# Stick-breaking mixer with query rows in the partitions and reversed scans for the later sums, in a two-layer streaming encoder

## Reference

```python
def sb_attend(q, q_pos, k, v):
    z = einsum('bqhd,bshd->bhqs', q, k) * HEAD_DIM ** -0.5
    strict = arange(n_keys)[None, :] < q_pos[:, None]
    log_keep = where(strict, log_sigmoid(-z), 0.0)
    later = cumsum(log_keep, axis=3, reverse=True) - log_keep
    weight = where(strict, exp(log_sigmoid(z) + later), 0.0)
    return einsum('bhqs,bshd->bqhd', weight, v)
```

## Time and profile before

| | |
|---|---|
| time, three runs | 1114.75 us median, 1114.19 to 1116.99 |
| profiled execution, first to last instruction | 1111.5 us |
| TensorE busy (matmul) | 1086.6 us, 98% |
| GpSimd, ScalarE, VectorE busy | 63%, 54%, 50% |
| mean granted TensorE clock | 0.998 |

### The profile page before, as it was taken

The page is one execution under the profiler, slowest core; times in us unless marked ns, Lnnn a source line. Parts: engine busy times, 40 slices in busy tenths (PEclk is TensorE's granted clock), DMA queues, the critical chain, the costliest instruction groups (busy, mean ns, idle before and its releaser), DMA issues.

```text
span 1111.5 us, 23055 instructions
## 1 busy us (share of the span) xinstructions
PE 1086.6 (98%) x8290; PEld 991.6 (89%) x8290; DVE 554.5 (50%) x1337; ACT 596.6 (54%) x1114; POOL 699.3 (63%) x319
## 2 busy tenths in 40 slices
PE   5999999999999999999999999999999999999996
PEld 2887888788899999999998788888999999999996
DVE  4557433455266755553247662454626775555212
ACT  3564545445447766565456544445554676565542
POOL 0874544445567887778877445444657788777882
PEclk9999999999999999999999999999999999999999
DMA  9955646756654355445566555574634435444541
GB/s 358 355 209 223 231 160 232 264 195 226 225 189 153 129 184 180 152 155 185 186 209 244 217 205 186 209 244 164 208 124 136 172 121 189 164 174 152 189 163 74
DMA packets 85695, 214.97 MB, mean 193 GB/s; under 512 B 13336, under 2 KB 33376, under 8 KB 85360
## 3 DMA queue, kind: packets, MB, share of 16 engines
q1 hardware_dynamic: 85616, 213.88, 54.1%
HBM read 208.80 MB, written 5.05 MB: 192 GB/s over the span
## 4 chain that ended last, share of the span: by engine, by line
PE 72%; issue 11%; POOL 8%; DVE 4%; DMA 2%; ACT 2%; SPq 1%; POOLq 0%; DVEq 0%; ACTq 0%
PE ps L720 11%; PE ps L716 11%; PE ps L717 11%; PE ps L755 8%; PE ps L756 7%; POOL wlo L596 7%; PE ps L757 7%; PE ps L652 2%; PE ps L708 2%; PE ps L707 2%; PE ps L706 2%; PE ps L1172 2%; DMA raw<-stream 1%; DVE hup L1737 1%; DMA first<-mod_first 1%
## 5 line engine op out<-in xcount | busy, mean ns | idle before, releaser
L596 POOL TENSOR_TENSOR wlo<-raw,whi 128x1024 fp32r<-128x1024 f32 x282 | 675.0, 2398 | 361.2 <-ACT whi L1266 303.3
L1266 ACT ACTIVATE whi<-raw 128x1024 fp32r<-128x1024 f32 x202 | 211.4, 1053 | 86.1 <-PE ps L720 62.6
L755 PE MATMUL ps<-hh,whi 128*128 128x288 f32 x816 | 249.3, 306 | 0.8 <-ACT gb L1348 0.6
L756 PE MATMUL ps<-hl,whi 128*128 128x288 f32 x816 | 241.8, 296 | 0.0
L757 PE MATMUL ps<-hh,wlo 128*128 128x288 f32 x816 | 241.3, 296 | 0.0
L755 PEld LDWEIGHTS ps<-hh,whi 128*128 128x128 f32 x816 | 153.7, 188 | 38.6 <-issue 35.5
L717 PE MATMUL ps<-ol,whi 128*128 128x290 f32 x576 | 156.9, 297 | 0.0
L716 PE MATMUL ps<-oh,whi 128*128 128x290 f32 x576 | 156.7, 297 | 0.0
L756 PEld LDWEIGHTS ps<-hl,whi 128*128 128x128 f32 x816 | 153.9, 189 | 0.0
L757 PEld LDWEIGHTS ps<-hh,wlo 128*128 128x128 f32 x816 | 153.7, 188 | 0.0
L716 PEld LDWEIGHTS ps<-oh,whi 128*128 128x128 f32 x576 | 108.9, 189 | 0.0
(11 more groups left out here) (289 smaller groups left out, 1914.6 us busy)
## 6 DMA issues: line engine op xcount, KB each, us to landing
raw<-stream SPq DMA_DIRECT2D x228, 512.0 KB, 4.3
mraw<-stream SPq DMA_DIRECT2D x40, 1024.0 KB
raw<-stream SPq DMA_DIRECT2D x88, 128.0 KB, 4.8
raw<-stream SPq DMA_DIRECT2D x24, 384.0 KB, 5.4
first<-mod_first SPq DMA_DIRECT2D x16, 512.0 KB, 11.5
raw<-stream SPq DMA_DIRECT2D x28, 256.0 KB, 5.0
o_proj<-proj SPq DMA_DIRECT2D x12, 288.0 KB
kvk<-keys_t SPq DMA_DIRECT2D x6, 512.0 KB, 3.8
```

The costliest lines, as they stand in the source:

```text
L596: nc.gpsimd.tensor_tensor(wlo[:, slot, :], raw[:, slot, :], whi[:, slot, :].bitcast(F32), ALU.subtract).then_inc(lo_ready, 1)
L755: mm(out, whi[:, slot, w], high, start=(i == 0), stop=False)
L756: mm(out, whi[:, slot, w], low, start=False, stop=False)
L1266: A(whi[:, slot, :], raw[:, slot, :], ACT.Copy).then_inc(hi_ready, 1)
```

## The change

Mixer D gets the layout of C and A. It becomes `D_ROWS`, the first of three users of `prompt_logits`, `sample_logits`, `turn_probs` and `values`; C and A become 1 and 2 and keep their slots. Its three parts are c = 0 (queries 0 to 127, four heads by 128 keys), c = 1 (queries 128 to 255, four heads by 256 keys) and c = 2 (the sample, 4 heads x 32 queries in the partitions by 544 keys). The sum over later keys is a `tensor_tensor_scan` that runs through the keys backwards, with a column of ones in PSUM as its multiplier. `z_soft_log`, `z_weights` and `mask_z` work on a whole part at once. The weights are then turned by `turn_probs` for the value products. The four late `swap`/`rotate` pairs move from slots 22, 24, 26, 28 (rotated at VectorE's 23, 25, 27, 29) to 17, 18, 20, 21 (rotated at 18, 19, 21, 22), so that bank 4 is free for the turned weights. Two masks are written over unused constants in the first layer. The rounds of `choose` keep their number.

```diff
-SWAP_AT = {4: (0, 1, 2), 22: (3,), 24: (4,), 26: (5,), 28: (6,)}
+SWAP_AT = {4: (0, 1, 2), 17: (3,), 18: (4,), 20: (5,), 21: (6,)}
...
                     if q == piece_at(32) + 5:
-                        sp.wait_ge(d_out, upto(l, d_out))
+                        sp.wait_ge(pv_done, upto(l, pv_done, 4))
...
                     if n == 3:
-                        pe.wait_ge(v_tok, upto(l, v_tok, 1))
+                        pe.wait_ge(vb_tok, upto(l, vb_tok))
                     elif n > 3:
                         pe.wait_ge(roped, upto(l, roped, n))
+                        if n == 5:
+                            pe.wait_ge(v_tok, upto(l, v_tok, 1))
...
                         pe.sem_inc(settled, 1)
+                        pe.wait_ge(roped, upto(l, roped, 5))
                         turn_rows(DV, 3, v_turned)
                     if t == 20:
-                        pe.wait_ge(kv_d_loaded, upto(l, kv_d_loaded))
                         pe.wait_ge(v_tok, upto(l, v_tok, 1))
-                        d_scores(0)
-                    if t == 21:
-                        pe.wait_ge(ol_ready, upto(l, ol_ready, 2))
-                        pe.wait_ge(v_tok, upto(l, v_tok, 1))
-                        for h in range(NH):
-                            j, r = h // 2, 64 * (h % 2)
-                            i = mm(ps[0:TS, 6 + h % 2, j * TS:(j + 1) * TS], proj[r:r + 64, DK + j, TP:T],
-                                   proj[r:r + 64, DQ + j, TP:T], start=(j == 0), stop=True, skip_group_check=True)
-                        i.then_inc(znew_ready, 1)
+                        prompt_logits(D_ROWS, 0, DQ, DK)
+                    if t == 22:
+                        pe.wait_ge(roped, upto(l, roped))
+                        turn_probs(D_ROWS, 0)
+                        prompt_logits(D_ROWS, 1, DQ, DK)
                     if t == 23:
-                        pe.wait_ge(znew_keep, upto(l, znew_keep))
-                        for b in range(2):
-                            i = mm(ps[0:TS, 6 + b, 0:2 * TS], cst[0:TS, C_NTRI:C_NTRI + TS], d_new[:, 0, b * 64:(b + 1) * 64],
-                                   start=False, stop=True, skip_group_check=True)
-                        i.then_inc(znew_logw, 1)
-                        d_log_weights(0)
-                    if t == 24:
-                        d_log_weights(1)
+                        values(D_ROWS, 0)
                     if t == 25:
-                        pe.wait_ge(wnew_ready, upto(l, wnew_ready))
+                        turn_probs(D_ROWS, 1)
+                        sample_logits(D_ROWS, DK)
                     if t == 26:
-                        d_scores(1)
-                        d_values(0)
-                    if t in (29, 30):
-                        d_log_weights(t - 27)
-                    if t == 32:
-                        d_values(1)
+                        values(D_ROWS, 1)
+                        turn_probs(D_ROWS, 2)
+                    if t == 27:
+                        values(D_ROWS, 2)
+                    if t == 28:
+                        turn_probs(D_ROWS, 3)
+                    if t == 29:
+                        values(D_ROWS, 3)
...
                         rows_out(3, v_tok)
+                        spread_queries(DQ)
                     if t == 21:
                         z_soft_log(0)
                     if t == 22:
-                        act.wait_ge(znew_masked, upto(l, znew_masked))
-                        soft_log(d_new[:, 0, :].rearrange("p (b n) -> p b n", b=2), znew, znew_log)
+                        z_weights(0)
+                    if t == 23:
+                        probs_out(D_ROWS, 0)
                         z_soft_log(1)
-                    if t == 24:
-                        act.wait_ge(znew_logw, upto(l, znew_logw))
-                        A(d_new[:, 1, :].rearrange("p (b n) -> p b n", b=2), znew, ACT.Exp).then_inc(wnew_ready, 1)
-                        z_weights(0)
                     if t == 25:
                         z_weights(1)
-                    if t in (27, 28):
-                        z_soft_log(t - 25)
-                    if t in (30, 31):
-                        z_weights(t - 28)
-                    if t == 33:
+                    if t == 26:
+                        probs_out(D_ROWS, 1)
+                        z_soft_log(2)
+                    if t == 27:
+                        probs_out(D_ROWS, 2)
+                    if t == 28:
+                        z_weights(2)
+                    if t == 29:
+                        probs_out(D_ROWS, 3)
+                    if t == 30:
+                        act.wait_ge(pv_done, upto(l, pv_done, 4))
                         for j in range(2):
-                            act.wait_ge(d_out, upto(l, d_out, j + 1))
-                            take_out(j, 6 + j)
+                            take_out(j, out_tile(D_ROWS) + j)
...
+                def later_sums(c):
+
+                    one = ps[:, (2, 4, 3)[c], 511:512]
+                    if c == 1:
+                        dve.wait_ge(probs_tok, upto(l, probs_tok, 1))
+                        in_order(V.memset(one, 1.0))
+                    dve.wait_ge(z_log, upto(l, z_log, c + 1))
+                    if c != 1:
+                        in_order(V.memset(one, 1.0))
+                    in_order(V.scalar_tensor_tensor(d_view(d_keep, c), z_view(c), 0.0, d_view(d_keep, c), ALU.max, ALU.add))
+                    parts, n = ((NH, P), (NH, TP), (1, PAST + TS))[c]
+                    for g in range(parts):
+                        back = slice((g + 1) * n - 1, g * n - 1 if g else None, -1)
+                        i = V.tensor_tensor_scan(d_later[:, back], one.broadcast_to([P, n]), d_keep[:, back], 0.0,
+                                                 ALU.mult, ALU.add)
+                    in_order(i)
+                    V.tensor_tensor(z_view(c), z_view(c), d_view(d_later, c), ALU.subtract).then_inc(logw_ready, 1)
...
+                    if t in (18, 19):
+                        rotate(t - 15)
                     if t in (17, 18):
                         choose(0, SEL_P // 2, t == 18)
...
                     if t == 21:
                         mask_z(0)
+                        rotate(5)
+                        later_sums(0)
+                    if t == 22:
+                        rotate(6)
                         choose(1, 1)
-                    if t == 22:
-                        dve.wait_ge(znew_ready, upto(l, znew_ready))
-                        z4 = znew.rearrange("p b (j n) -> p b j n", j=2)
-                        V.tensor_tensor(z4, z4, strict[0:TS, 0:TS].unsqueeze(1).unsqueeze(1).broadcast_to([TS, 2, 2, TS]), ALU.add).then_inc(znew_masked, 1)
+                    if t == 23:
                         mask_z(1)
-                        keep(0)
-                    if t == 23:
-                        dve.wait_ge(znew_log, upto(l, znew_log))
-                        V.scalar_tensor_tensor(keep_new, znew, 0.0, keep_new, ALU.max, ALU.add).then_inc(znew_keep, 1)
-                        keep(1)
-                        rotate(3)
+                        choose(1, 1)
                     if t == 24:
-                        choose(1, 2)
-                    if t == 25:
-                        rotate(4)
+                        later_sums(1)
+                    if t == 26:
+                        mask_z(2)
+                        choose(1, 1)
                     if t == 27:
-                        mask_z(2)
-                        mask_z(3)
-                        rotate(5)
-                    if t == 28:
-                        keep(2)
+                        later_sums(2)
+                    if t in (28, 29, 30):
                         choose(1, 1)
-                    if t == 29:
-                        keep(3)
-                    if t == 29:
-                        rotate(6)
-                    if t in (30, 31):
-                        choose(1, 2, t == 31)
-                    if t == 33:
+                    if t == 30:
                         for j in range(2):
-                            take_low(j, 6 + j, 2 + j)
+                            take_low(j, out_tile(D_ROWS) + j, 2 + j)
+                    if t == 31:
+                        choose(1, 2, True)
```

More of the change, by code:

```diff
@@ L386, in encoder @@
         f_log = signal("f_log", 1)
-        queries_ready = signal("queries_ready", 2)
+        queries_ready = signal("queries_ready", 3)
         sigmoided = signal("sigmoided", 4)
-        logits = signal("logits", 6)
+        logits = signal("logits", 9)
         max_ready = signal("max_ready", 6)
         exp_ready = signal("exp_ready", 6)
[L392 to L395, removed]
+        probs_ready = signal("probs_ready", 9)
+        turned = signal("turned", 12)
+        probs_tok = signal("probs_tok", 12)
+        pv_done = signal("pv_done", 12)
         dots = signal("dots", 2 * IH + 2)
@@ L472, in up_bank, with out_tile, z_view, d_view @@
```

(32 more changed lines are left out.)

145 lines of the change are left out of this document (49 added, 96 removed).

## The result

The changed kernel takes 1104.18 us (median of four runs, 1103.61 to 1105.18), the kernel before on the same chip 1114.47 us. The profiled execution has a span of 1101.8 us against 1111.5 before, 9.7 us less. One execution of the experiment `before_no_sums` had a granted clock of 0.754 and took 1293.98 us; no time or ratio in this text uses it.

The account below looks back on a forecast made before the run. TensorE was taken to bound the kernel: 6.5 us net gain a layer, 13.0 in all, less 4.2 of waits, gives 8.8 us off 1114.75, so 1105.9 us; range 1100.5 to 1111.

Parts of the forecast that it names:

- TensorE's net gain: Mixer D's stage, slots 17 to 32: 15.70 us removed, 8.68 added, 0.5 for breaks, so 6.5 us less per layer.
- Logits: Mixer D's prompt logits on TensorE, priced from mixer C's rows: 0.84 us against 128 keys, 1.26 against 256, per layer.
- Moved swaps: Late swaps in earlier TensorE slots: same 0.57 us each wherever they stand; three more breaks between tiles, 0.5 us per layer.
- The scan price: VectorE's later sums: low price taken, 0.34 us for 128 elements, 0.68 for 256, 1.45 for 544.
- one SBUF operand, so not held: VectorE's new scans read ones from PSUM, so GpSimd's splits, which block two SBUF operands, do not stop them.
- My evidence from `keep`: VectorE's `keep`, the nearest row with one SBUF operand, stayed at 669 to 693 ns over eight; supports the low price.
- the long chains: Rival C: reversed scans on VectorE cost more, waits of 6.4 us a layer eat the gain, 1114.5 us; chance 0.09.
- the scans held by GpSimd: Rival D: splits hold VectorE's scans, waits of 10.8 us a layer, slower at 1123 us; chance 0.06.
- the high price: VectorE's scans at 6.3 ns an element, from one long scan: 0.81, 1.6 and 3.4 us for 128, 256, 544 elements.
- The waits: TensorE waits for rotations held by GpSimd's split: 1.1 us in slot 18, about 1.0 in slot 22, 2.1 per layer.
- rival B: The splits don't meet the rotations, so TensorE has no waits: gain 13.0 us, 1101.7 us; chance 0.23.
- Slot 25 in time: Turning of part 1 on TensorE: 12.6 us after its logits, chain 10.9 and up to 1, in time by about 1.

Follow-up runs that it names:

- before_no_sums: The kernel before without the triangle and block matmuls of the sums over later keys, only the new keys' kept: 1098.81 us, ratio 0.9866.
- the doubled one: The changed kernel with every scan of the later sums run twice, same result: 1104.26 us, ratio 0.9908 to the kernel before.
- psum_operand: The changed kernel, its four late rotations' second instruction reading PSUM instead of the cosines in SBUF: 1098.85 us, ratio 0.9859 to the kernel before.
- free banks: The changed kernel with the swaps of slots 18 and 21 in PSUM banks 2 and 7, so without both waits: 1098.43 us, ratio 0.9852 to before.

## Why the prediction was right

**The mechanism held in every step; two sizes were off, and their errors nearly cancel.** A microsecond of TensorE work in the stage was a microsecond of the end; two waits came, in slots 18 and 22; both were the rotation's second instruction, held by a split; no other wait came. The windows were forecast at 73.5 us busy of 75.6 and read 73.09 of 75.42.

**TensorE's net gain: forecast 6.5 us a layer, measured 7.44.** The terms by the rows:

- Logits were 0.40 too dear. They took 0.64 (123.75 to 124.39) and 1.06 (134.27 to 135.33), forecast 0.84 and 1.26. The price was twice that of two heads in C, where the 8-row matmuls of the decay lie between two pairs of heads; D's eight run on without them.
- Moved swaps were 0.5 too dear. I took 0.57 each and a break of 0.15 besides. Alone in a tile, in slots 17 and 21, one costs 0.48: two products follow in 0.75 us (107.77 to 108.52 in the timeline) where two take 0.27.
- Turnings were forecast 0.2 too cheap: 0.59, 0.53, 0.58 and 0.63 against 4 x 0.53. The last has five blocks.
- What went was 0.19 more. The new keys' sums (L1113), for which I had no row, took 0.34 (135.47 to 135.81), not 0.25. The sums of the first head, right behind them, took 2.33 (135.81 to 138.14), not 2.23:

```profile
135.47 0.41 PE L1113 MATMUL ps<-d_new,cst 32*32 32x64 f32 x4
135.81 1.13 PE L875 MATMUL ps<-d_keep,cst 128*128 128x512 f32 x2
...
138.14 0.40 PE L755 MATMUL ps<-hh,whi 128*128 128x288 f32 x1
```

These come to 0.40 + 0.48 - 0.21 + 0.19, 0.86 of the 0.94. The large term, 8.92 us for the sums, was confirmed within 0.2 by dropping most of them.

**The scan price: right.** Low prices 0.34, 0.68 and 1.45 us; measured 0.34 (from one start to the next), 0.66 and 1.29. No scan met a hold, in the change or in the doubled one, with splits running beside them (part 1's four, from 140.84 to 143.27 in the change, beside that of 141.38 to 143.78). The step "one SBUF operand, so not held" was shown twice: by the scans, and by `psum_operand`, where the same substitution frees an instruction that was held. My evidence from `keep` was thinner than it read: of its eight rows only two ran beside a split for more than 0.01 us, for 0.5 us each. The measured prices and durations rule out the long chains and the scans held by GpSimd. Doubling the scans adds 1.4 and 2.4 us to parts 0 and 1, less than the 1.8 and 3.8 of the high price, and used up the room in both. At the high price some 0.4 and 1.4 us would be left over, an estimate from these differences: about 1.8 us of waits more a layer, where the rival had 4.3 (6.4 against 2.1). So its 1114.5 us would not have come even then, but some 1108. For slot 22, its sum added the length of a chain to a wait whose end is that of a split.

The Trainium skill, "SBUF — State Buffer", section "Who interferes with whom", calls the shared port pair "an exclusive lock". The 0.32 us from the end of a split to the end of each held instruction, and the 453 to 455 ns of all eight with one SBUF operand, agree with it.

**The waits: forecast 1.1 and 1.0 us, cost 1.49 and 1.31.** The positions were right within 0.5 us: `rotate(3)`'s second instruction was put at 110.65, its end at 112.5 (it came at 110.95 and 112.34), `rotate(6)`'s 8.6 us behind the end of tile 20, in a split (it came 8.1 behind, at 131.29 against 123.17). The price of a wait was mis-sized. I counted the idle time, and the list of waits shows 1.2 and 1.1. But the swap at 112.97 lies 1.50 us behind the last product at 111.47, and with free banks the swap follows at 0.14 (111.47 to 111.61): 1.36. The first matmuls behind the wait are slower too, 0.66 to the next group (112.97 to 113.63) against 0.57 with free banks: 1.45 together. In slot 22 it is 1.41 less 0.13, and 0.59 against 0.53: 1.34. The list shows 0.2 to 0.3 us less for each wait than it takes. It counts from the end of the last product's record, 0.30 us long, where the next matmul would have started 0.13 or 0.14 behind its start.

**The sum.** Net gain 0.94 above the forecast and waits 0.7 above it, a layer: two mis-sized terms that nearly cancel, 4.64 against 4.4, and that is luck. The forecast 8.8 us stands against 9.3 in the stages, with 0.4 more between them. The time came 1.7 us below the forecast, and 0.9 of it is this; the rest is the distance from the profiled span to the median, put at 3.25 us and here 2.4.

**The time fell below rival B's once its condition held.** B said 1101.7 us with no waits. The version with no waits took 15.4 us less than before instead of B's 13.0: the net gain was too small by 1.9 us in two layers, and 0.4 lies outside the stages.

**Slot 25 in time: right, by 1.8 us where I had said about 1.** In the change's timelines of ScalarE and TensorE the exponential is over at 146.19 and the turning starts at 148.00:

```profile
145.18 1.01 ACT L1332 ACTIVATE probs<-ps 128x1024 f32<-128x1024 f32 x1
...
148.00 0.60 PE L645 MATMUL ps<-cst,probs 128*128 128x128 f32 x4
```

With 2.4 us more of scans that room is used up to the last 0.05 us.

**VectorE's work.** I had some 8 us more for mixer D; its rows come to about that (scans 5.1, subtractions 2.7), and the rest of the 12.0 is held rotations and other work in the window. It cost nothing by itself, as forecast.

## What to carry to other kernels

When a step moves from TensorE to VectorE, look which SBUF operands its instructions read and what GpSimd does at that moment. In the change's trace 563 VectorE instructions with a PSUM operand start inside a split, 0.3 us or more before its end, and none is held. When a wait comes from a buffer and not from the data, another bank is cheaper than another order; here it gave 5.6 us, more than half of what the change itself gave. Do not add a longer chain to a wait before you have found what ends it: below that end it costs nothing, and shortening it may let an instruction slip past a collision.

## What was not expected of the hardware

Counting SBUF inputs is not enough. In the kernel before, the `tensor_scalar` that ends a search of `choose` reads one operand, in SBUF, and writes SBUF; it takes 0.30 us in the change, where no split runs beside it, and here 2.24:

```profile
169.53 2.38 POOL L596 TENSOR_TENSOR wlo<-raw,whi 128x1024 fp32r<-128x1024 f32 x1 [2.49 <-ACT whi L1266]
...
169.81 2.24 DVE L1865 TENSOR_SCALAR score<-score 128x256 f32<-128x256 f32 x1
```

The prediction's "one SBUF operand, so not held" is right for the scans and for `rotate`, which have a PSUM operand besides; it is not a rule for any instruction with one SBUF input.

Two more things:

- A wait of TensorE costs more than its idle time in the list: two of 1.2 and 1.1 us cost 1.45 and 1.34, of which 0.06 to 0.09 is the slower first group behind it and the rest what the list doesn't count. The one of 0.22 us cost 0.46.
- A scan costs the same backwards over 128 partitions as forwards over 8: 0.66 us for 256 elements here, 0.68 in the earlier trace rows. It takes 1.29 us for 544 elements where a `scalar_tensor_tensor` of the same 544 takes 0.72. The Trainium skill, "DVE: opcode table, instruction layouts, handler registers and perf-mode slots", section "6. Datapath and trigger behaviour", says that the built-in scan "runs at half throughput". The two rows agree with it roughly, 1.8 to 1, and by the step in length, 2.1 ns an element (128 to 544) against 1.1 (0.69 us for 512, 1.23 for 1024), more closely.
